# Where the operands of the matmuls begin in SBUF: three paddings changed, everything else the same

## The reference

```python
proj = h @ w_in[l]
...
mixed = g_a * (o_a @ w_up_a[l]) + g_b * (o_b @ w_up_b[l]) + g_c * (o_c @ w_up_c[l])
x = x + mixed @ w_out[l]
h = rms_norm(x, ffn_norm[l])
x = x + (jax.nn.silu(h @ w_ffn_gate[l]) * (h @ w_ffn_up[l])) @ w_ffn_down[l]
```

## Time and profile before

| what | value |
|---|---|
| time of the kernel before, median of 3 runs | 1053.38 us (1052.88 to 1055.06) |
| the profiled execution, its own time | 1054.85 us |
| span of the profiled execution | 1053.1 us |
| PE busy | 1038.6 us (99%) |
| PEld busy | 1010.4 us (96%) |
| DVE busy | 741.8 us (70%) |
| ACT busy | 579.7 us (55%) |

### The profile page before, as it was taken

One profiled execution on the slowest core, in us unless ns is written; L12 is line 12 of the kernel. 1 busy time (PEld: TensorE's weight loads), 2 busy tenths in 40 slices (PEclk: granted clock), 3 DMA queues, 4 the chain that ended last, 5 costly groups with the idle time before them and its releaser, 6 DMA issues.

```text
span 1053.1 us, 22212 instructions
## 1 busy us (share of the span) xinstructions
PE 1038.6 (99%) x8760; PEld 1010.4 (96%) x8760; DVE 741.8 (70%) x1098; ACT 579.7 (55%) x880; POOL 77.2 (7%) x92
## 2 busy tenths in 40 slices
PE   8999999999999999999999999999999999999998
PEld 7899899999999999999999999898889999999998
DVE  6699888747876666657666667667986876665666
ACT  5456755576565544556544445455666665554453
POOL 0000000001310000111000001041001300000110
PEclk9999999999999999999999999999999999999999
DMA  6356433345556554655655466464435555554663
GB/s 230 135 171 221 160 106 141 120 144 182 195 182 219 190 185 147 202 201 192 209 193 197 143 199 218 169 206 159 149 121 195 180 190 196 199 206 140 201 222 120
DMA packets 32444, 187.81 MB, mean 178 GB/s; under 512 B 3832, under 2 KB 7552, under 8 KB 14720
## 3 DMA queue, kind: packets, MB, share of 16 engines
q1 hardware_dynamic: 31472, 185.58, 50.7%
q0 software_dynamic: 416, 1.06, 0.4%
q10 hardware_dynamic: 496, 0.33, 0.1%
HBM read 184.98 MB, written 1.06 MB: 177 GB/s over the span
## 4 chain that ended last, share of the span: by engine, by line
PE 82%; DVE 10%; ACT 2%; issue 1%; DMA 1%; DVEq 0%; ACTq 0%
PE acc L683 77%; DVE wlo L1577 3%; PE area_a L683 2%; PE area_t L683 2%; DVE score L1807 1%; DMA raw<-in_w_bi 1%; DVE work L1820 1%; DVE st L1818 1%; ACT whi L1181 0%; DVE s_sum L2135 0%; ACT he L1181 0%; PE area_t L949 0%; ACT s_a L1181 0%; DVE mask L1782 0%; DVE st L1767 0%
## 5 line engine op out<-in xcount | busy, mean ns | idle before, releaser
L683 PE MATMUL acc<-hs,whi 128*128 128x256 f32 x3584 | 618.6, 278 | 6.5 <-DVE wlo L1577 5.5
L683 PEld LDWEIGHTS acc<-hs,whi 128*128 128x128 f32 x3584 | 539.9, 187 | 14.2 <-issue 9.8
L683 PE MATMUL acc<-hs,wlo 128*128 128x256 f32 x1792 | 495.1, 276 | 0.0
L1181 ACT ACTIVATE whi<-raw 128x1024 fp32r<-128x1024 f32 (+3 forms) x379 | 357.0, 978 | 160.0 <-PE acc L683 117.1
L1577 DVE TENSOR_TENSOR wlo<-raw,whi 128x1024 fp32r<-128x1024 f32 (+4 forms) x259 | 272.4, 1093 | 96.8 <-ACT whi L1181 95.8
L683 PEld LDWEIGHTS acc<-hs,wlo 128*128 128x128 f32 x1792 | 335.7, 187 | 0.2
L683 PE MATMUL acc<-hid,whi 128*128 128x256 f32 x1056 | 180.2, 276 | 0.3 <-DVE wlo L1577 0.3
L683 PEld LDWEIGHTS acc<-hid,whi 128*128 128x128 f32 x1056 | 159.0, 188 | 0.7 <-DVE wlo L1577 0.5
L683 PE MATMUL acc<-hid,wlo 128*128 128x256 f32 x528 | 145.8, 276 | 0.0
L1665 DVE TENSOR_TENSOR wlo<-raw,whi 128x1024 fp32r<-128x1024 f32 x120 | 141.1, 1217 | 4.7 <-ACT whi L1181 4.7
L1678 DVE TENSOR_TENSOR hbuf<-acc,sbuf 128x256 f32<-128x256 f32 x66 | 28.0, 424 | 114.1 <-PE acc L683 110.7
(11 more groups left out here) (316 smaller groups left out, 1025.2 us busy)
## 6 DMA issues: line engine op xcount, KB each, us to landing
raw<-in_w_gu SPq DMA_DIRECT2D x66, 1024.0 KB, 4.8
raw<-in_w_dn SPq DMA_DIRECT2D x48, 704.0 KB, 4.1
raw<-in_w_up SPq DMA_DIRECT2D x10, 1024.0 KB, 4.8
raw<-in_w_gates1b SPq DMA_DIRECT2D x8, 1024.0 KB, 4.8
raw<-in_w_out SPq DMA_DIRECT2D x8, 1024.0 KB, 4.8
raw<-in_w_qk SPq DMA_DIRECT2D x8, 1024.0 KB, 4.9
raw<-in_w_gates SPq DMA_DIRECT2D x8, 1024.0 KB, 4.9
raw<-in_w_projT_b SPq DMA_DIRECT2D x7, 1024.0 KB, 4.7
```

The lines of the kernel that those rows point to most:

```text
L683: return nc.tensor.matmul(out, w, m, start=start, stop=stop, skip_group_check=True)
L1181: return nc.scalar.activation(out, in_, f, **kw)
```

## The change

Two lines. One adds 64 bytes ahead of `whi`, the other makes the padding behind `wlo` 256 bytes where it was 128. No instruction is added, removed or moved, no transfer changes its size, and the order and the waits on each engine are those of before.

```diff
         x = fixed("x", (KD, T))
         raw = fixed("raw", (2, SLOT))
+        top[0] += 64
         whi = fixed("whi", (2, SLOT), F32R)
         top[0] += 128
         wlo = fixed("wlo", (2, SLOT), F32R)
-        top[0] += 128
+        top[0] += 256
         tmp = fixed("tmp", (4, T))
         con = fixed("con", (N_CONST,))
```

## The result

| | before | after |
|---|---|---|
| median of 4 runs each | 1053.68 us (1052.88 to 1055.06) | 1084.31 us (1083.65 to 1085.98) |
| ratio of the times | | 1.0292, 95% interval 1.028 to 1.0305 |
| span of the profiled execution | 1053.1 us | 1084.2 us |

The change made the kernel slower by 2.9%. The forecast of no change was wrong, and the time lies outside its range.

What follows compares the result with a forecast made beforehand. The prediction took PE's stream of 7,344 256-column matmuls to bound the kernel. Every term was 0, so the 1053.1 us span stayed and it forecast the earlier median, 1053.4 us, range 1040 to 1063 us (0.83).

Steps and rivals of the forecast that it cites:

- The forecast of no change: Whole kernel: the change does nothing measurable, median 1053.4 us, with about 2.1 us as the limit of detection; chance 0.62.
- What bounds the kernel: PE's stream of 7,344 256-column matmuls at 113.35 ns, 832 us of the 1053.1 us span; one nanosecond each is 7.3 us.
- The weights, from 128 and 0 to 192 and 64: Main stream's weight starts: `w_fvl` rows show both placements at 117 ns each, so the new residues cost 0 us.
- The moving operand, from 64 to 0: Main stream: 512-column rows bound a slowdown at 0.35 to 2 ns per matmul, 2.6 to 14.7 us; taken as 0.
- The swapped matmuls: 156 matmuls of `w_bi`, `w_sv` and others, moving operand `whi` or `wlo`: at most 0.6 us; taken as 0.
- the splits: ACT and DVE writing `whi` and `wlo` from `raw`: new residues already in the trace at like speed; taken as 0.
- transfers: Weights land in `raw` and output leaves from `x`, neither moving; constants stay at multiples of 32 bytes; 0.
- The slower rival: Main stream: moving operand reads slower from start 0, 0.35 to 2 ns per matmul, 1056 to 1068 us; chance 0.19.
- its variant of 4 ns per matmul: Main stream: the loss paid once per matmul, not per column, 29 us, 1083 us; chance one in fifty.
- its sign of recognition: In the profile after, the mask at 0 above 230 ns and `w_bi` at 192 and 64 below it, trading places.
- The faster rival: Main stream: new placing removes part of the excess over 106.7 ns, 1046 to 1051, 1038 or 1029 us; chance 0.19.
- the 6.7 ns: Main stream's excess per matmul over 106.7 ns, 256 columns at one per cycle; at most 49 us to win.

Runs made afterwards that it cites:

- m2_fine: Separate test kernel, 48-matmul runs: one weight buffer at every 16 bytes of distance, plus 8 and 64 weight columns; 128-column paces 113.3 to 120.2 ns.
- e1: Against the kernel before, only the weights move, high to 192 and low to 64, moving operand staying at 64; 1086.71 us.
- m1_map: Separate test kernel, 48-matmul runs in groups of high, high, low, with weights at chosen distances from the moving operand; settled paces 113.3 to 120.0 ns.
- m4_lead: Separate test kernel: 48-matmul runs behind a lead matmul of varied length, paces 113.3 to 118.9 ns; also 8 to 128 weight columns, 60 to 111.6 ns.
- m3_shapes: Separate test kernel, one weight buffer, varying moving columns, distance and type; 256 columns pace 113.3 to 120.0 ns in float32r, 109.17 in bf16.
- e3: The kernel before with weights and moving operand all shifted by 192, to high 64, low 192, moving operand 0; 1054.21 us.
- e4: The changed kernel with weights and moving operand shifted by 64, to high 0, low 128, moving operand 64; 1082.95 us.
- e5: Against the kernel before, only the change's first line, 64 bytes ahead of the high weights, moving all operands by 64; median 1053.26 us, ratio 0.9998.

## Why the prediction was wrong

**What bounds the kernel** was right: the stream of 256-column matmuls, worth 7.3 us for each nanosecond on the 7,344, and the loss came out of it alone.

**The step that failed is *The weights, from 128 and 0 to 192 and 64*.** It said that the position of the weights relative to the moving operand "has little to act on" and that "the change only swaps which buffer has which", and took 0 us. Measured, the swap is worth 5.57 ns for each of 6,515 matmuls, and the kernel is 30.6 us slower. Four things were wrong with it:

- *The rows were no sample of the stream.* The earlier trace rows showed 117 ns in both halves, not the stream's 113.3, and that should have been the warning. There are only six such matmuls between 512-column ones, and a run before could take up to 13 to settle; in `m2_fine` the same shape, given 48, has paces from 113.3 to 120.0 by distance and start. Equal numbers of an unsettled run said nothing of the settled one: in the profile after, these matmuls still take 117 ns each, while the stream is at 118.9.
- *The rows didn't hold the new placing.* The prediction said that "the trace holds both placements", which is true of the starts and not of the distances. In the earlier trace rows the moving operand stays at 64, so the weights of the second half, at 192 and 64, lie at the distances 128 and 0. That is the placing of e1, which took 1086.71 us, and neither the old pair (64, 192) nor the new one (192, 64).
- *The two buffers are not alike.* A group of three uses the high weights twice and the low ones once. The chain's mean was a mean over the pair (64, 192), and said nothing of (192, 64). In `m1_map` and `m4_lead` the first always settles at 113.3 and the second at 118.9 in 22 of 28 starts.
- *That the weight loads "steal" nothing* was concluded from the 8 columns. `m4_lead` shows that float32r loads of 128 columns let the stream go no faster than 111.6 ns. A moving column costs (226.7 - 173.3) / 128 = 0.417 ns at distance 0 in `m3_shapes`, so 256 of them need about 106.7 ns by an estimate from these rows. At 256 columns, then, both streams last almost the whole interval. `m3_shapes` fits: with fewer columns the load alone sets the pace and the distance is without effect. By the Trainium skill, TensorE: Matmul & The Clock Gate, section LDWEIGHTS, a load takes its columns divided by 1.2 in nanoseconds, an estimate of 106.7 for 128. The runs agree with that slope (0.83 ns a column), and the stream that the load holds back is 4.9 ns above the figure. That the two meet in reading SBUF is an argument, not shown; weights of 8 columns, at 113.3 to 120.0 ns, speak against it in its simple form.

***The moving operand, from 64 to 0*** was rightly taken at 0: e3 has it at 0 and takes 1054.21 us. Its bound from 512-column rows had no force, since there the order of the distances is another (`m3_shapes`). ***The swapped matmuls***, ***the splits*** and ***transfers*** were 0, as the rows of `w_bi`, ACT and DVE after show.

**The slower rival** had the sign, and its variant of 4 ns per matmul, 1083 us, came within 2 us of the result. That was luck: it charged 4 ns to every matmul for the moving operand's start, and its mechanism fell with e3 and e4, and its sign of recognition too: the mask at 0 took 0.91 us and `w_bi` the same 6.23. **The faster rival** asked for a placing that wins back part of the 6.7 ns; none of the distances in `m1_map` and `m2_fine` paces under 113.3 ns. By the Trainium skill, TensorE: Matmul & The Clock Gate, section Back-to-back issue gap, 256 columns take 262 cycles at 2.4 GHz, 109.2 ns. In bf16 the chip agrees with that figure (109.17 ns in `m3_shapes`); in float32r no run of 256 columns here settles below 113.3.

What the prediction didn't have is the **class** of effect: it asked what each matmul costs at an address, and the stream has paces into which it locks. A kernel's time is then set by which runs lock where: after, 21 of 49 runs were fast, but both runs of 1,584 were slow.

**Open.** Which event at a run's start, or within it, picks the pace, why 64 for the high and 192 for the low weights leads all runs to the fast one, and by what path the distance acts. No version beat the kernel before.

## What to carry to other kernels

In a float32r kernel whose stream is 128 weight columns by 256 moving columns, place the weights at a chosen distance modulo 256 from the moving operand, and measure the pace: here 64 above for the weights that are used twice and 64 below for the others gave 113.3 ns in every start and every run that was measured, other placings up to 120. Treat paddings between such buffers as tuned numbers, and after any change of the memory map read the gap between starts in several long runs, not the busy time or the mean duration, which hardly show it. When a short stretch of the trace is to stand for a long one, first see that it has the long one's pace.

## What the runs showed of the hardware that was not expected

- A stream of equal matmuls has more than one stable pace with the same operands: 113.3 or 118.9 ns at (192, 64), held for up to 1,584 matmuls. The pace is mostly taken in the first matmuls of a run, but one run of 240 in e4 went over after its 192nd. At (192, 64) three of four starts behind a lead matmul of 192 columns were fast, none behind one of 240.
- Of the addresses only the distance modulo 256 was seen to count: a shift of all operands by 64 (e5, ratio 0.9998) or by 192 (e3, 1054.21 us) changes nothing, and 256 more of distance doesn't either (three cases in `m1_map`, 113.3 ns).
- The effect depends on length and type: under 0.5 ns up to 240 columns, 113.3 to 120.0 ns at 256, the opposite order at 512 (226.7 at distance 0, 233.2 at 64), none in bf16.
